# Gate products per head on stacked halves of u, and another order of one round, in a hybrid diffusion backbone

## The reference

```
z = h_lat @ w_in                      # u, g, f, gf: four slabs of 1024 columns; zc for the context
u = centred_depthwise_conv(u, w_conv, b_conv)        # 4 taps
for d in range(2):                    # forward, backward
    r = sigmoid(block_diag_linear(u, w_a[d], b_a[d]))     # 16 heads of 64 x 64
    i = sigmoid(block_diag_linear(u, w_x[d], b_x[d]))
    log_a = -8 * r * softplus(-lam[d])
    a, b = exp(log_a), sqrt(-expm1(2 * log_a)) * (i * u)
    h = linear_scan(a, b, h0)         # context first, then latent with the context's last state
y_r = (h[0] + h[1]) * silu(g)
y_f = (fft2(f).real @ w_f + b_f) * silu(gf)          # over tokens and channels of a group
y = concat(y_r, y_f) @ w_out
```

## Time and profile before

| what | value |
|---|---|
| median of 3 runs | 1395.48 us (1395.1 to 1396.59) |
| the profiled execution, its own time | 1395.62 us |
| its span, first to last instruction | 1393.8 us |
| PE busy | 1342.8 us (96%) |
| PE weight loads busy | 1139.1 us (82%) |
| DVE, ACT, POOL busy | 1017.8, 763.6, 466.7 us |
| mean granted clock of TensorE | 0.992 of full speed |

### The profile page before, as it was taken

One profiled execution on the slowest core, in us unless ns is written; L12 is line 12 of the kernel. 1 busy time (PEld: TensorE's weight loads), 2 busy tenths in 40 slices (PEclk: granted clock), 3 DMA queues, 4 the chain that ended last, 5 costly groups with the idle time before them and its releaser, 6 DMA issues. The chain is left out here.

```text
span 1393.8 us, 20353 instructions
## 1 busy us (share of the span) xinstructions
PE 1342.8 (96%) x7116; PEld 1139.1 (82%) x7116; DVE 1017.8 (73%) x1446; ACT 763.6 (55%) x1230; POOL 466.7 (33%) x231
## 2 busy tenths in 40 slices
PE   5999999999999999999999999999998999999998
PEld 4787888888888888877888888878786888888786
DVE  6789969696969696885346457679864899998732
ACT  5465646464646465673122224443344899999421
POOL 0022323232323232312345342013201666667543
PEclk9999999999999999999999999999999999999999
DMA  9323231313131313255675764555699533252694
GB/s 374 150 97 102 79 104 60 103 60 103 60 103 60 103 60 104 62 217 201 198 250 195 235 233 167 196 181 171 192 255 276 191 110 88 83 154 78 184 266 126
DMA packets 107807, 210.29 MB, mean 151 GB/s; under 512 B 11840, under 2 KB 60512, under 8 KB 105440
## 3 DMA queue, kind: packets, MB, share of 16 engines
q1 hardware_dynamic: 107744, 209.48, 46.1%
HBM read 151.76 MB, written 57.69 MB: 150 GB/s over the span
## 5 line engine op out<-in xcount | busy, mean ns | idle before, releaser
L1065 PE MATMUL slab<-h_hi,w_hi 128*128 128x512 f32 x720 | 256.4, 356 | 3.4 <-DVE h_lo L404 2.6
L1066 PE MATMUL slab<-h_lo,w_hi 128*128 128x512 f32 x720 | 255.7, 355 | 0.0
L1067 PE MATMUL slab<-h_hi,w_lo 128*128 128x512 f32 x720 | 255.3, 355 | 0.0
L1037 POOL TENSOR_TENSOR w_lo<-wraw,w_hi 128x1024 fp32r<-128x1024 f32 x29 | 78.3, 2698 | 300.6 <-ACT w_hi L657 300.6
L1065 PEld LDWEIGHTS slab<-h_hi,w_hi 128*128 128x128 f32 x720 | 136.5, 190 | 23.2 <-DVE h_lo L404 2.9
L2894 POOL TENSOR_TENSOR probs<-probs,rdenom 128x2560 f32<-128x2560 f32 (+1 forms) x32 | 135.7, 4242 | 53.0 <-DVE rdenom L2842 53.0
L1067 PEld LDWEIGHTS slab<-h_hi,w_lo 128*128 128x128 f32 x720 | 136.5, 190 | 19.2
L1066 PEld LDWEIGHTS slab<-h_lo,w_hi 128*128 128x128 f32 x720 | 136.6, 190 | 18.9
L2863 DVE TENSOR_TENSOR pt_lo<-TB,pt_hi 128x512 fp32r<-128x512 f32 x152 | 103.8, 686 | 21.8 <-ACT pt_hi L2802 17.2
L2763 ACT ACTIVATE probs<-probs,neg_max 128x640 f32<-128x640 f32 (+1 forms) x128 | 102.7, 802 | 11.7 <-DVE neg_max L2834 9.4
L2834 DVE CUSTOM_DVE_ANT_0 probs<-S,mask,nsink 128x640 f32<-128x640 f32 (+1 forms) x128 | 107.5, 843 | 2.1 <-PE S L2925 2.1
(11 more groups left out here) (411 smaller groups left out, 3503.3 us busy)
## 6 DMA issues: line engine op xcount, KB each, us to landing
wraw<-in_w_in SPq DMA_DIRECT2D x32, 512.0 KB, 3.5
wm<-in_wm SPq DMA_DIRECT2D x32, 512.0 KB, 3.6
early<-in_w_in SPq DMA_DIRECT2D x26, 512.0 KB, 4.0
mixT<-work SPq DMA_DIRECT2D x16, 640.0 KB, 4.0
wm<-in_wm SPq DMA_DIRECT2D x8, 1024.0 KB, 16.0
mraw<-mixT SPq DMA_DIRECT2D x16, 512.0 KB, 7.6
w_sum<-early SPq DMA_DIRECT2D x16, 512.0 KB, 3.4
w_raw<-w_sum SPq DMA_DIRECT2D x16, 512.0 KB, 5.1
```

The costliest lines, as they stand in the source:

```text
L1037: sub(w_lo[:, j % 2].rearrange("p k n -> p (k n)"), wraw[:, j % 2, :], v32(w_hi[:, j % 2].rearrange("p k n -> p (k n)")), ALU.subtract).th ...
L1065: nc.tensor.matmul(out, l_hi, r_hi, start=start, stop=False)
L1066: nc.tensor.matmul(out, l_hi, r_lo, start=False, stop=False)
L1067: return nc.tensor.matmul(out, l_lo, r_hi, start=False, stop=stop)
```

## The change

It concerns rounds 1 to 7 alone; round 0 keeps its products and its order.

- Two tiles `u_parts` take the place of u_hi and u_lo, one for each head. Tile 0 holds u_hi of head 0 on partitions 0 to 63 and u_lo of head 0 on 64 to 127; tile 1 holds u_hi of head 1 on 64 to 127 and u_lo on 0 to 63. The weights are laid out so that both halves of a column hold the same head's 64 rows, and a product's 128 outputs are matrix a and matrix x of one head. A product is two matmuls, gw_hi and gw_lo by `u_parts`, in place of three.
- ACT makes the hi parts in two copies of 64 partitions; the lo parts are two subtractions on DVE, where POOL had one.
- A product now holds halves of A and of B, so ACT reads each in two activations of 64 partitions (`read_halves`): 12 for a direction, not 6. The gate weights are loaded with 128 KB in each of two DMAs, 64 KB before.
- On PE the first GF chunk stands before the last two products of the forward direction, and the first G chunk before the last two of the backward one; then comes G's 256-token chunk, the DFT product and G's second chunk.
- On ACT the hi part of slab G's weights and ab_hi stand between the fourth and fifth product of the forward direction; two of the GF tanhs stand before the root and the third behind it; pq_hi stands between the exponentials; all G tanhs stand before the second root, y_hi behind the first.
- On DVE the sums of block 0 stand behind the convolution, one on each side of the two subtractions, and the last two sums before the backward direction's products; the G products stand before the second scan. In round 7 the weights of steps 1 and 2 and `mixed_lo(1, 0)` stand behind that scan.

The core of the diff:

```diff
+        u_parts = [sb("u_parts0", [P, T], F32R), sb("u_parts1", [P, T], F32R)]
+        u_hi, u_lo = u_parts
+        HALF = (slice(0, HEAD), slice(HEAD, P))
...
+                    for rows in HALF:
+                        sp.dma_start(gw[rows, :, rows], a["w_gate0"][rows]).then_inc(gw_ld, 16)
                 else:
                     sp.wait_ge(gwl, t)
-                for c in range(2):
-                    sp.dma_start(gw[HEAD * c:HEAD * (c + 1), :, HEAD * c:HEAD * (c + 1)],
-                                 a["w_gate"][t, HEAD * c:HEAD * (c + 1), :, :]).then_inc(gw_ld, 16)
+                    for rows in HALF:
+                        sp.dma_start(gw[rows], a["w_gate"][t]).then_inc(gw_ld, 16)
...
+            def read_halves(t, d, between):
+                for head in range(2):
+                    to = HALF[head]
+                    for c, (at, n) in enumerate(CHUNKS):
+                        k = 6 * d + 3 * head + c
+                        if k == 4:
+                            between()
+                        act.wait_ge(gp_, 12 * t + k + 1)
+                        for x, dst in enumerate((A, B)):
+                            col = C_HALF + 2 * x + d
+                            nc.scalar.activation(dst[to, at:at + n], W[HALF[head ^ x], k % 4, 0:n], ACT.Tanh, scale=0.5,
+                                                 bias=cur[to, col:col + 1]).then_inc(gr, 1)
+
+            def gates(t, d, first, reading=None, between=None):
...
+                    read_halves(t, d, reading)
+                    act.wait_ge(gr, read_before(t, False) + 12 * d + 12)
                 if d == 0:
                     act.wait_ge(mp, 4 if first else 2 * N_MOD * t + 6)
                 else:
                     act.wait_ge(bt, 2 * t + 1)
+                    if not first:
+                        act.wait_ge(mp, 2 * N_MOD * (t + 1))
...
+                        ab_high()
+
+                    def pq_and_first_mix():
+                        pq_high()
+                        if last:
+                            mixed_hi(0, 0)
+
+                    gates(t, 0, False, second_slab_and_ab)
+                    silu_gf(t, False, (0, 1))
+                    root(t, 0)
+                    silu_gf(t, False, (2,))
+                    y_high()
+                    if not last:
+                        split_hi(t + 1, SLAB_U)
+                    gates(t, 1, False, lambda: None, pq_and_first_mix)
+                    tanh_g(t, (0,), False)
+                    if last:
+                        weight_hi(0)
+                    tanh_g(t, (2, 1), False)
+                    root(t, 1)
+                    if last:
+                        weight_hi(1)
+                        mixed_hi(1, 0)
+                        weight_hi(2)
...
                     silu_gf(0)
                 dve.wait_ge(conv, 2 * t + 2)
                 if not first:
+                    mod_sums(t, 0, E, (0,))
+                    for head, rows in enumerate(HALF):
+                        dve.wait_ge(uh, 2 * t + head)
+                        nc.vector.tensor_tensor(u_parts[head][HALF[1 - head]], u[rows], v32(u_parts[head][rows]),
+                                                ALU.subtract).then_inc(ul, 1)
+                    mod_sums(t, 0, E, (1,))
                     mod_sums(t, 1, E)
                     mod_sums(t, 2, E)
...
+                    silu_g(2)
+                else:
+                    silu_gf(0)
+                    silu_gf(1)
+                    scan(0)
+                    silu_gf(2)
+                    y_low()
+                    dve.wait_ge(om, 2 * t + 1)
                     mod_sums(t, 3, E)
-                scan(1)
-                if last:
+                    direction(1)
+                    pq_low()
                     silu_g(0)
-                    weight_lo(0)
+                    if last:
+                        weight_lo(0)
+                    silu_g(2)
                     silu_g(1)
-                    weight_lo(1)
-                    mixed_lo(1, 0)
-                    silu_g(2)
-                    weight_lo(2)
-                else:
-                    for c in (2,) if first else range(3):
-                        silu_g(c)
+                    scan(1)
+                    if last:
+                        weight_lo(1)
+                        mixed_lo(1, 0)
...
+                    pool.wait_ge(uh, 1)
+                    sub(u_lo[:], u[:], v32(u_hi[:]), ALU.subtract).then_inc(ul, 1)
                 split_lo(t, SLAB_G)
...
                             u_hi[:, at:at + n], u_lo[:, at:at + n], True, True).then_inc(gp_, 1)
+
+            def gate_products(t, d, products):
+                for i in products:
+                    head, c = i // 3, i % 3
+                    at, n = CHUNKS[c]
+                    k = 6 * d + i
+                    if k in (0, 3):
+                        pe.wait_ge(ul, 2 * t + head)
+                    if k < 3:
+                        pe.wait_ge(xr, 3 * t + k + 1)
+                    elif k > 3:
+                        pe.wait_ge(gr, read_before(t, False) + 2 * (k - 3))
+                    out, parts = W[:, k % 4, 0:n], u_parts[head][:, at:at + n]
+                    nc.tensor.matmul(out, gw_hi[:, 2 * d + head, :], parts, start=True, stop=False)
+                    nc.tensor.matmul(out, gw_lo[:, 2 * d + head, :], parts, start=False, stop=True).then_inc(gp_, 1)
 
...
-                pe.wait_ge(ul, t + 1)
-                gate_products(t, 0)
                 if first:
+                    pe.wait_ge(ul, 1)
+                    first_gate_products(0)
                     slab_product(t, SLAB_G, True, (0, 1))
+                    first_gate_products(1)
+                    dft_product(t, True)
+                    slab_product(t, SLAB_G, True, (2,))
                 else:
-                    slab_product(t, SLAB_GF, False)
-                gate_products(t, 1)
-                dft_product(t)
-                slab_product(t, SLAB_G, first, (2,) if first else range(3))
+                    gate_products(t, 0, range(4))
+                    slab_product(t, SLAB_GF, False, (0,))
+                    gate_products(t, 0, (4, 5))
+                    slab_product(t, SLAB_GF, False, (1, 2))
+                    gate_products(t, 1, range(4))
+                    slab_product(t, SLAB_G, False, (0,))
+                    gate_products(t, 1, (4, 5))
+                    slab_product(t, SLAB_G, False, (2,))
+                    dft_product(t, False)
+                    slab_product(t, SLAB_G, False, (1,))
                 pe.wait_ge(pql, t + 1)
...
     w0 = slabs(g["l0_w_in"])
-    w_gate = np.stack([g["l0_w_a"][0], g["l0_w_x"][0], g["l0_w_a"][1], g["l0_w_x"][1]])
+    wa, wx = (g["l0_w_" + n].reshape(2, KT, 2, HEAD, HEAD) for n in "ax")
```

165 lines of the change are left out of this document (81 added, 84 removed).

## The result

The changed kernel takes 1413.77 us, the median of four runs (1411.11 to 1415.89), against 1396.03 (1395.1 to 1397.28) of the kernel before in the same series: 1.3% slower, ratio 1.0133 with an interval of 1.0114 to 1.0151. The forecast was 1399.3 and the range ended at 1404.5, so the sign was right and the size far off. The profiled execution has a span of 1414.1 us against 1393.8, and its mean granted clock is 0.982 against 0.992.

A forecast was written before the change was run, and what follows sets the result against it. PE, busy for all 69.8 us of a round, was taken to bound the kernel. Saving 7 x 0.4 = 2.8 us and losing 6.6 at the projection gave +3.8 on 1395.62, so 1399.4, forecast as 1399.3; range 1392.5 to 1404.5.

The forecast's parts named there:

- What PE saves: Gate products of rounds 1 to 7: one matmul of three goes from each of twelve, 2.30 us a round.
- The chain to the backward reads: ACT and DVE work up to the backward gate reads: reads begin at u = 52.1, DVE 0.6 us later than ACT.
- the load's wait: DVE in a later round: idles about 1 us until block 2's load lands at u = 33.2.
- The half reads: ACT's gate reads: a 64-partition read costs as much as a whole one, 0.57 us for 512 tokens, 0.36 for 256.
- Together 1.9 of the 2.3 us go back, and a round gains 0.4: PE's waits at the fifth and sixth backward products return 1.9 us; 0.4 a round stays, 2.8 in seven.
- Seven rounds alike: Rounds 1 to 7: taken as alike, the seventh up to its end, each gaining 0.4 us.
- The end of round 7: Projection start: second root and scan stand behind the last tanh, PE waits 5 us, step 6 comes 6.6 us later.
- The load takes longer: Rival, block 2's load in each round: each 0.1 us over 3.6 costs 0.1 a round, 1401.5 to 1407; chance 0.14.
- ACT's chain alone: Rival, later rounds: ACT alone binds, waits of 0.6 and 0.7, gain 1.0 a round, 1395.2 us; chance 0.20.
- The end is hidden: Rival, projection: its later waits absorb the 6.6 us, giving 1392.8 us; chance 0.10.
- no wait is left: Rival, later rounds: half reads cost half, all 2.30 us a round stay, giving 1386.1 us; chance 0.08.

The follow-up runs named there:

- experiment 5: Kernel before's order with two-matmul products and half reads: 1455.8 us; changed kernel's order with three-matmul products and six whole reads a direction: 1398.85 us.
- the order alone: Changed kernel's order with the kernel before's gate products: three matmuls on whole parts, six whole reads a direction, one subtraction; 1398.85 us.
- experiment 2: Changed kernel with both sums of block 0 ahead of the two subtractions of u on DVE; 1407.06 us.
- Experiments 1: Changed kernel with ten and five matmuls without use on PE ahead of the fifth and sixth backward products in rounds 1 to 7; 1402.11 us.
- experiments 3 and 4: Changed kernel with six whole reads a direction, 1386.55 us; changed kernel with backward products 4 and 5 behind G chunks 0 and 2, 1395.41 us.
- experiment 6: Changed kernel with round 7's second root, backward scan and silus of G back in the kernel before's sequence; 1413.42 us.

## Why the prediction was wrong, step by step

- **What PE saves, 2.30 us a round.** Right. From start to start the six products of a direction take 1.71 and 0.69 us in the changed kernel's forward direction, 2.51 and 1.03 with three matmuls in the same order (experiment 5): 1.14 a direction. With whole reads a round is 1.84 us shorter; the order alone leaves it at 69.67.
- **The chain to the backward reads.** Right in its structure and nearly in time. In round 4 (start 335.12) the reads begin at u = 52.7, forecast 52.1; the root starts at 381.70, u = 46.6, forecast 46.0; the fifth forward product is read from u = 36.8, as forecast; the load's wait is 1.29, forecast about 1; DVE stood for POOL. The two subtractions cost 1.5 each, not 1.4. DVE and ACT are half a microsecond apart, as forecast: experiment 2 makes DVE earlier, and ACT's chain takes over. PE comes to the fifth backward product at u = 52.8, forecast 52.3.
- **The half reads.** The wrong term in the chain. I argued that a half read costs what a whole one does and then took 0.57 and 0.36, the distances of whole reads, which overlap by about 0.1 us. The half ones don't: 0.71 and 0.49. The figure of the Trainium skill (ScalarE: Activation LUTs, What ACT_TABLE_LOAD costs) which I had quoted beside, 0.28 us + 0.833 ns per element, gives 0.71 and 0.49 as an estimate, which is what the trace shows; the same page of the Trainium skill adds that activations in a row overlap by some 93 ns, which the trace shows for whole reads and not for these. Four backward reads take 2.9 us and not 2.3. The first stop costs 1.44 us from start to start, forecast 1.2, and the second 0.95, forecast 0.6; together 2.4 against 1.9. By this alone a round would have been 0.1 us longer than before instead of 0.4 shorter, and 0.5 longer with the delay of 0.4 at G's first chunk, for which the forecast had no term. Measured without the half clock: 69.8 with the earlier sums, 69.97 in round 1, 70.3 with fillers.
- **No term for the clock.** The failed step. "Together 1.9 of the 2.3 us go back, and a round gains 0.4" took a stop of PE to cost its own length. In six of seven rounds it costs another 1.5 us at half clock, 9 us of the 14.5 by which the forecast missed; most of the rest is the half reads. The profile of before could have warned, outside the rounds. PE's stops of 1.47 us at 626.88 and of 1.72 at 660.42 have no half clock behind them, but one of 2.09 us in layer 1 has (the row, then the table by stretch):
```profile
916.48 0.47 PE L2554 MATMUL slab<-h_t,w_s 128*128 128x512 f32 x1 [2.09 <-ACT q_halves L2159]
```
```profile
917.10:920.50 3.40, 3.40 (x10) 2.65 (x9) 3.40 (x3) 0.79 (x2) 1.29 (x1) 0.50 0.18 36
```
A stop could thus cost more than its length, and none of the terms or rivals had it. Experiments 1 and 2 show the price, 1.5 and 1.47, experiments 3 and 4 that it goes with the stop.
- **Seven rounds alike.** Wrong for round 1: it took 71.71 before and takes 69.97 after, a gain of 1.7 that I hadn't looked for. The new order takes away what lengthened it (69.88 with the order alone; before, PE waits 0.73 and 0.49 us in it). That no half clock falls in it in this execution is luck, as experiment 2 shows. The gain hides part of the loss: rounds 2 to 7 lose 12.0.
- **The end of round 7.** The size was right, 6.36 measured against 6.6, and the wait of 4.94 for DVE's weight at step 1 was forecast at 5. The wait of 1.07 for DVE at step 6 says that DVE's queue set the time, as reckoned. The cause was only half right. I read it as the place of root and scan behind the last tanh; undoing just that (experiment 6) gives nothing back. What costs is that the whole backward direction ends late in the new order, since G's chunks, which covered it, are spent as fillers; the order alone shows it with whole reads, and putting all of round 7 back removes it. The backward scan ends 64.4 us after the start of round 7 before and 77.1 after.
- **The rivals.** "The load takes longer" had the right direction for another reason; the load's wait came as forecast, and taking it away (experiment 2) left PE's waits at 1.7 us. That experiment is also the case of "ACT's chain alone": the waits are then 1.0 and 0.7 and not 0.6 and 0.7, and no gain comes. "The end is hidden" and "no wait is left" are out. None of the four had the clock in it, and so the range had no end for it.
- **The sum.** Round 1 starts 0.3 us earlier and is 1.7 shorter; the other six lose 12.0, 9 by the clock and 3, half a microsecond each, by what the stops (2.4 us at the late products and 0.4 at G's first chunk) cost beyond the saved products. The end of round 7 loses 6.4. Together 16.3 of the 20.3 between the two profiled executions.

## What to carry to other kernels

A stop of a matmul engine that is full costs more than its length: where a change trades busy matmuls for a wait in the same place, price the wait also with a stretch at half clock behind it, count how often it recurs, and look for other matmuls that can stand there. Two matmuls saved are worth nothing if what reads their result takes longer than the work put between; here 2.9 us more of filler ahead of two products were worth 18 us, and with that, the earlier sums and the last round left as it was, the change gives 1389.2 us, 0.45% less than before. When work is moved forward to fill gaps in a loop, look at what it covered at the loop's end: the last round may want the old order.
